# The FFN's up product as seven Strassen products, with weight parts formed on the fly

## The reference, cut to what matters

```python
def conv_glu_ffn(h, w_up, conv_w, conv_b, w_down):
    u = h @ w_up                       # 2048x1024 @ 1024x5632
    u = conv over 3 tokens, channel by channel, of u, + conv_b
    a, b = jnp.split(u, 2, axis=-1)    # 2816 channels each
    return (jax.nn.gelu(a, approximate=True) * b) @ w_down   # 2816x1024

x = x + rmsnorm(mix @ w_out, g_mix_post)
f = conv_glu_ffn(rmsnorm(x, g_ffn_pre), w_up, conv_w, conv_b, w_down)
x = x + rmsnorm(f, g_ffn_post)
```

## Time and profile before

| | us |
|---|---|
| median of 3 runs | 3394.72 (3394.04 to 3396.75) |
| profiled execution, its own time | 3392.44 |
| its span, first to last instruction | 3390.7 |
| PE busy | 3274.3 (97%) |
| DVE, ACT, POOL busy | 1412.9, 1190.6, 603.1 |
| mean granted TensorE clock | 0.989 |

### The profile page before, as it was taken

How to read it: one execution, slowest core, us unless ns; L and a number is a source line. 1 busy time by engine, 2 the same in 40 slices (tenths; PEclk the granted TensorE clock), 3 DMA queues, 4 the chain that set the end, 5 groups by cost and what they waited for, 6 DMA issues and landing times. The chain is left out here.

```text
span 3390.7 us, 46499 instructions
## 1 busy us (share of the span) xinstructions
PE 3274.3 (97%) x16834; PEld 2657.2 (78%) x16834; DVE 1412.9 (42%) x3866; ACT 1190.6 (35%) x2459; POOL 603.1 (18%) x551
## 2 busy tenths in 40 slices
PE   7999999998998989999999999999999999999998
PEld 6888888887776766666678878887888788888887
DVE  5111101105766977777744454304440344115421
ACT  5111111115666866666633343203330233013310
POOL 1566654530000014442110000000000000000000
PEclk9999999998999999999999999999999999999999
DMA  5789976657878833442247775646556655665553
GB/s 192 268 315 323 326 257 216 215 179 192 213 174 200 206 89 77 102 102 62 74 138 240 237 262 191 248 169 254 197 203 233 233 190 198 238 246 193 192 197 138
DMA packets 299259, 676.10 MB, mean 199 GB/s; under 512 B 99392, under 2 KB 154944, under 8 KB 284864
## 3 DMA queue, kind: packets, MB, share of 16 engines
q1 hardware_dynamic: 265344, 517.80, 48.0%
q0 software_dynamic: 33696, 155.40, 12.7%
HBM read 495.93 MB, written 185.57 MB: 201 GB/s over the span
## 5 line engine op out<-in xcount | busy, mean ns | idle before, releaser
L543 PE MATMUL z_banks<-h_hi,z_w_hi 128*128 128x512 f32 x972 | 381.2, 392 | 0.0
L543 PE MATMUL z_banks<-h_hi,z_w_lo 128*128 128x512 f32 x972 | 378.4, 389 | 0.0
L1640 PE MATMUL banks<-low,f_own 128*128 128x512 f32 x1344 | 312.6, 392 | 12.8 <-issue 6.6
L1640 PEld LDWEIGHTS banks<-low,f_own 128*128 128x128 f32 x1344 | 254.1, 189 | 67.2 <-issue 14.1
L1424 ACT ACTIVATE w_small<-w_small,a_stats 128x128 f32<-128x128 f32 (+3 forms) x510 | 257.1, 517 | 109.4 <-DVE a_stats L1510 80.8
L1354 PE MATMUL a_ot_ps<-a_turned_w,vs 128*64 128x256 f32 (+3 forms) x1452 | 221.3, 428 | 0.0
L1321 PE MATMUL a_t_ps<-idt,w_small 128*128 128x128 f32 x1092 | 216.2, 284 | 4.7 <-DVE a_turned_w L1413 2.6
L323 ACT ACTIVATE st_hi<-z_banks 128x512 fp32r<-128x512 f32 (+1 forms) x100 | 59.8, 598 | 444.2 <-PE z_banks L543 318.8
L461 DVE TENSOR_TENSOR st_lo<-z_banks,st_hi 128x512 fp32r<-128x512 f32 x76 | 52.3, 691 | 384.1 <-ACT st_hi L323 307.9
L543 PEld LDWEIGHTS z_banks<-h_hi,z_w_lo 128*128 128x128 f32 x972 | 182.6, 188 | 37.0
L543 PEld LDWEIGHTS z_banks<-h_hi,z_w_hi 128*128 128x128 f32 x972 | 182.7, 188 | 36.9
(11 more groups left out here) (263 smaller groups left out, 7081.9 us busy)
## 6 DMA issues: line engine op xcount, KB each, us to landing
f_own<-f_hi SPq DMA_DIRECT2D x88, 512.0 KB, 3.7
f_own<-f_lo SPq DMA_DIRECT2D x88, 512.0 KB, 4.6
z_xs<-in_w_ffn POOLq DMA_DIRECT2D x33, 1024.0 KB, 8.1
f_hi<-z_v_hi POOLq DMA_DIRECT2D x33, 1024.0 KB, 5.1
f_lo<-z_xs POOLq DMA_DIRECT2D x33, 1024.0 KB, 5.7
low<-z_hi SPq DMA_DIRECT2D x48, 512.0 KB, 7.7
k_hi<-f_hi SPq DMA_DIRECT2D x44, 512.0 KB, 3.6
k_hi<-f_lo SPq DMA_DIRECT2D x44, 512.0 KB, 4.5
```

The lines of the kernel that those rows point to most:

```text
L543: last = pe.matmul(banks[:, 4 * k + n, :], w[:, k, c, :], h[c][:, tok], start=(c == order[0] and q == 0), stop=(c == DC - 1 and q == 2))
L1640: last = pe.matmul(out, w[:, c * P:(c + 1) * P], rows[:, c, :], start=(c == 0 and x == 0), stop=(c == DC - 1 and x == 2))
```

## The change

- `split_v` and its DMAs leave `project`. `mix_out` and `ffn` become one function, `mix_ffn`, one block without loops in the program.
- The FFN goes through two halves of 1024 tokens (hf). Per channel tile, A is the 2x2 split of the weights (a or gate channels by upper or lower 512 of the model width) and B the 2x2 split of the tokens' rows (512 of width by 512 tokens). Seven products of 12 matmuls each take the place of eight (`PRODUCTS`). n = hf*22 + j numbers the channel tiles, so there are 44.
- For each n, GpSimd forms the four sums S1 to S4 of the raw weights and the lower parts of all seven operands, in eight instructions (`form`); ScalarE forms the upper parts in four. The raw 128x2048 tile comes by one DMA. The sums of rows T1 to T4 and their parts are formed once per half by VectorE and ScalarE.
- VectorE joins the products out of PSUM in five additions of 512 columns (`add_p6`, `add_p7`, `add_p5`, `take_c21`, `take_c12`), ScalarE copies P1 and C11. Taps, gelu and gate are as before, but 1024 columns long.
- Gated rows are stored in DRAM (`g_up`) and loaded again for the down product; w_down is loaded raw, and ScalarE and VectorE form the parts of both in each step (`split_down`). Six places, as before; the last two d, not four, are ordered by token tile.
- The rows h2 of tokens 1024 to 2047 go to DRAM unsplit (`h2_rest`) and are loaded by GpSimd in the first half's down product.

```diff
+PRODUCTS = ((0, A11, B11, True, 1, 1), (1, S2, T2, True, 2, 2), (0, A12, B21, False, 1, 3), (2, S3, T3, True, 3, 5),
+            (3, S1, T1, True, 3, 4), (2, A22, T4, False, 4, 6), (3, S4, B22, False, 4, 7))
...
+            def sums_a(n):
...
+                else:
+                    pool.wait_ge(p_done, 7 * (n - 1))
+                pool.tensor_tensor(lo[:, S1], raw[:, 2], raw[:, 3], ALU.add).then_inc(s_done, 1)
+                pool.tensor_tensor(lo[:, S3], raw[:, 0], raw[:, 2], ALU.subtract).then_inc(s_done, 1)
+                pool.wait_ge(s_done, 4 * n + 1)
+                pool.tensor_tensor(lo[:, S2], lo[:, S1], raw[:, 0], ALU.subtract).then_inc(s_done, 1)
...
+            def form(n):
+                raw = raws[n % 2]
+                sums_a(n)
+                lower_a(n, A11, 2, raw[:, 0:2], 1)
+                sum_b(n)
+                lower_a(n, S1, 2, None, 3)
+                lower_a(n, S3, 2, None, 4)
+                lower_a(n, A22, 1, raw[:, 3:4], 2)
...
+            for hf in range(2):
+                n0 = hf * NF
+                for n in range(n0 + (hf == 0), n0 + NF):
+                    last = n == n0 + NF - 1
+                    if not last:
+                        upper_a11(n + 1)
+                    if n > n0:
+                        last_tap(n - 1, 0, tap_a)
+                    take_p1(n)
+                    if n > n0:
+                        gelu(n - 1)
...
+                        upper_a22(n + 1)
+                        upper_s12(n + 1)
+                    take_c11(n)
...
+                        upper_s34(n + 1)
+                    last_tap(n, 1, tap_b)
...
+            def add_p7(n):
+                if n == 0:
+                    dve.wait_ge(h_turned, NT)
+                elif n == NF:
+                    dve.wait_ge(stored[1], 16 * TILES)
...
+                    if n > n0:
+                        tap(n - 1, 0, 1)
+                        tap(n - 1, 0, 0)
+                    add_p6(n)
+                    if n > n0:
+                        gate(n - 1)
...
+                    add_p7(n)
...
+                    add_p5(n)
...
+                    edge(n, 1)
...
+                    take_c21(n)
+                    tap(n, 1, 1)
+                    take_c12(n)
+                    edge(n, 0)
+                    tap(n, 1, 0)
...
+            def product(n, i):
...
+                if i == 2:
+                    pe.wait_ge(e1_done, n + 1)
+                elif i == 5:
+                    pe.wait_ge(ev_done, 5 * n + 2)
+                elif i == 6:
+                    pe.wait_ge(ev_done, 5 * n + 3)
+                w_hi, w_lo = a_hi(n, a)[:, 0, :], a_lo(n, a)[:, 0, :]
+                for c in range(4):
+                    for x, (w, rows) in enumerate(((w_hi, b_hi[b]), (w_lo, b_hi[b]), (w_hi, b_lo[b]))):
+                        last = pe.matmul(banks[:, 4 * (n % 2) + bank, :], w[:, c * P:(c + 1) * P], rows[:, c * 512:(c + 1) * 512],
```

The order at the two places where the FFN's halves begin. At the start (n = 0), ScalarE's queue and VectorE's queue around the last two token tiles of the mixer:

```diff
+                take_h(t - 1)
...
+                if t == NT - 1:
+                    upper_b(0, 2)
+                    upper_b(0, 3)
+                    upper_a11(0)
+                    upper_a22(0)
+                    upper_s12(0)
+                    upper_s34(0)
+            root_mix(NT - 1)
+            upper_b(0, 4)
+            take_p1(0)
+            root_x1(NT - 1)
...
+            act.wait_ge(h2_done, NT)
+            upper_b(0, 5)
+            take_c11(0)
+            upper_b(0, 6)
+            upper_a11(1)
...
+                if t == NT - 1:
+                    lower_b(0, 2)
+                    lower_b(0, 3)
+            to_x1(NT - 1)
+            lower_b(0, 4)
+            to_h2(NT - 1)
```

Between the halves, GpSimd's queue (q == 1, tiles t0 = 4 to 7, n = NF = 22):

```diff
+                        sums_a(NF)
+                        statistics(t0)
+                        lower_a(NF, A11, 2, raw[:, 0:2], 1)
+                        statistics(t0 + 1)
+                        sum_b(NF)
+                        lower_a(NF, S1, 2, None, 3)
+                        statistics(t0 + 2)
+                        lower_a(NF, S3, 2, None, 4)
+                        lower_a(NF, A22, 1, raw[:, 3:4], 2)
+                        store(t0)
+                        statistics(t0 + 3)
+                        for t in range(t0 + 1, t0 + TILES):
+                            store(t)
```

More of the change, by code:

```diff
@@ L1623, in _ @@
                     finish((n - 10) // 4)
[L1626 to L1642, removed]
@@ L1645, in mix_out @@
[L1645 to L1662 removed]
+NF = 22
@@ new lines @@
+LAST = 2
+TILES = 4
+SLOTS = 6
+HALF = T // 2
+STEPS = 2 * NF
+A11, A12, A22, S1, S2, S3, S4 = range(7)
+B11, T3, B21, B22, T1, T2, T4 = range(7)
+PRODUCTS = ((0, A11, B11, True, 1, 1), (1, S2, T2, True, 2, 2), (0, A12, B21, False, 1, 3), (2, S3, T3, True, 3, 5),
+            (3, S1, T1, True, 3, 4), (2, A22, T4, False, 4, 6), (3, S4, B22, False, 4, 7))
+SPLIT_ORDER = (B11, T2, B21, T1, T3, T4, B22)
+SUM_AT = {18: 0, 19: 1, 20: 2, 27: 3}
+UPPER_AT = {26: 0, 28: 1, 29: 2, 30: 3, 31: 4, 32: 5, 33: 6}
@@ L1976, in ffn @@
         rstd_done = sem("rstd_done")
+        gp_in = sem("gp_in")
+        r_in = [sem("r_in0"), sem("r_in1")]
         f_taken = sem("f_taken")
@@ L2016, in store @@
+                if t % 8 < 6:
                     pool.wait_ge(stored[t % 2], 16 * (t // 2) + 16)
                     load_x(t + 2)
[L2019 to L2035 removed]
+            split_lower(pool, 0)
@@ new lines, in project @@
+            def project(t):
+                k = t % 2
+                pe.wait_ge(ol_done, t + 1)
+                if t >= 2:
+                    pe.wait_ge(y_done, t - 1)
+                by_row = t in (0, NT - 1)
+                for n, c in [(n, c) for c in range(DC) for n in range(2)] if by_row else \
+                        [(n, c) for n in range(2) for c in range(DC)]:
+                    if t == 0 and n == 0:
+                        pe.wait_ge(wlo_done[c % 2], c // 2 + 1)
+                    for i, (part, w) in enumerate(((0, 0), (1, 0), (0, 1))):
+                        last = pe.matmul(mix[:, k, n * 512:(n + 1) * 512], oo[:, k, part, c, :], w_part(w, c)[:, n, :],
+                                         start=(c == 0 and i == 0), stop=(c == DC - 1 and i == 2))
+                    if t == NT - 1 and c == 3 and n == 1:
+                        last.then_inc(front_used, 1)
+                last.then_inc(mixed, 1)
@@ new lines, in _ @@
+            turn_o(0)
+            keep_turning(pe, banks[:, 6, :], idt, 16)
+            for t in range(NT):
+                if t + 1 < NT:
+                    turn_o(t + 1)
+                project(t)
+                if t:
+                    turn_h(t - 1)
+            for hf in range(2):
+                for n in range(hf * NF, hf * NF + NF):
+                    for i in range(7):
+                        product(n, i)
+                        if n == 0 and i == 3:
+                            turn_h(NT - 1)
+                for qq in range(2):
+                    down(hf, qq)
```

1125 lines of the change are left out of this document (668 added, 457 removed).

## The result

The changed kernel took 3315.88 us (median; 3312.45 to 3316.46), the kernel before beside it 3395.73. The ratio is 0.9762, 95% interval 0.9746 to 0.9779: 80 us faster, where 72 were forecast (3323 us). The profiled execution's span is 3310.7 us.

The account below looks back on a forecast made before the run. TensorE's queue, busy 97%, was taken as the bound. Matmuls -119.7, laps +21.2, start +14.1, between halves +8.0 and end +4.4 sum to -72.0, giving 3323 us; range 3286 to 3385.

Parts of the forecast that it names:

- its own sign of being wrong: Mid-half laps of 19.04 us, TensorE's own time for one n, would show the forecast of about 19.6 wrong.
- The matmuls: Up product: 528 fewer matmuls at 0.2267 us each, -119.7 us.
- the ring of 19.57 us: Up-product lap: turns of GpSimd, VectorE and ScalarE take 19.57 us against TensorE's 19.04, costing +21 us over forty laps.
- rival (a): Up-product laps: TensorE stays the bound in every lap, the turns fit in 19.04 us; 3292 us, chance 0.24.
- GpSimd's wait for ScalarE: Up-product lap: GpSimd idles 1.75 us for ScalarE's upper parts of A22 and S1/S2, with VectorE's gate running under it.
- The 0.5, 0.9, 1.4 us of growing lag: Up-product laps: GpSimd's S1 starts this far behind TensorE's product 0 in successive laps, until product 5 waits.
- the 4.8 and 4.9 us of lag: Start of each half: the next form late beyond the steady lag, 4.8 us in the first, 4.9 in the second.
- The start: FFN start: late operand parts, late next form and half clock lose 21.9 us, +14 us net.
- Between the halves: Turn between halves: add_p7 of n = 22 waits for tile 7's store; 8.4 us gap, 16.3 lost, +8 us net.
- The quarter boundaries: Down product: transfers and splits fit under its steps, taken as free, 0 us.
- The end: Kernel's end: only two last d in token order, so x1 of tile 15 is issued later, +4.4 us.
- The rival on the other side: Up-product laps: VectorE waits for a whole GpSimd operation each time, 22.0 us per lap, 3419 us; chance 0.12, or worse.

Follow-up runs that it names:

- e8: Changed kernel with product 0 of each n run twice (12 more matmuls, the first 12 overwritten): 3424.93 us, ratio 1.0092.
- e10: Changed kernel with two more GpSimd subtractions per form, and the taps' first operand read from PSUM except in each half's last n: 3313.73 us, ratio 0.9757.
- e6: Changed kernel with one more GpSimd subtraction of 512 columns in each of the 44 forms: 3345.36 us, ratio 0.9857.
- e7: Changed kernel with two more GpSimd subtractions in each form: 3406.33 us, ratio 1.0039 to the kernel before.
- e4: Changed kernel with ScalarE forming the first upper parts at the FFN's start before taking h2 of tile 14, not after: 3307.36 us, ratio 0.9749.
- e3: Changed kernel with GpSimd issuing stores of tiles 4 to 7 between the halves as soon as ready, x1 loads after the next lower part: 3305.10 us.
- e12: Changed kernel with the second half's third raw weight tile loaded only when the store of tile 7 has landed: 3309.35 us, ratio 0.9747.
- e2: Changed kernel with the down product's last four d, not two, in token order in all quarters but the second: 3303.32 us, ratio 0.9734.
- e9: Changed kernel with early upper parts, early stores, last four d by token, and the last tile's addition behind two splits at quarter boundaries: 3284.33 us.
- e11: Changed kernel with the second half's third raw weight tile loaded only when tile 7 is added up: 3313.54 us, ratio 0.9758.

## Why the prediction was right, and where its steps were not

The time came out 7 us under the forecast and inside the range, but the mechanism that the forecast rested on was not the one that ran: its own sign of being wrong, laps of 19.04, is what the trace shows. That the total fits is luck, as said above.

**The matmuls.** -119.7 us: right, and shown by the unbroken pieces and by e8, where the same number of matmuls, 528, cost 112.

**The lap.** The step that failed is the ring of 19.57 us; rival (a), laps of 19.04, is what the chip did. Its parts were good: GpSimd's 512 columns took 1.29 us (1.25 taken), the exclusion lengthens GpSimd's instruction by about 1.0 (1.15 taken), and e10 shows that it counts. In the changed kernel's lap the rows up to the end of S4 come to 10.2 us without the 0.5 of the fourth tap (10.29 in the sum), the wait for ScalarE to 1.5 (1.75) and the last three lower parts to 6.0 (6.1). What the sum had too long is its end: the last tap in full, 1.15, of which S1 felt 0.5, and the copies, 0.3, of which it felt nothing. Without its 0.8 us of waiting for TensorE the lap is 18.2 us.

Wrong above all was to hold GpSimd's wait for ScalarE (1.75 us, with the gate under it) fixed when GpSimd runs late. That wait exists while GpSimd is early. When it falls behind, the taps stand before other instructions of its own, the parts are ready when it comes, and 0.15 us of the wait are left (e6), while the gate comes to stand in GpSimd's way. So the bound is the sum that rival (a) named, GpSimd's instructions and VectorE's five, forecast at 18.5 and inferred from e6 and e7 as 18.4 (19.71 - 1.33). The 0.5, 0.9, 1.4 us of growing lag came from the same mistake. It cost the forecast all of the 21 us: of the 2.3 measured, 1.7 are the clock in 1973 to 1983. It also cost part of the 4.8 and 4.9 us of lag at the halves' begins.

**The start.** 18.0 lost, 21.9 forecast; product 0 began 10.7 us behind the last mixer matmul, forecast 10.8, and product 5 at 28.7, forecast 29.0. Right, for the reason given; e4 shows ScalarE's order to be it. The 3 us for half clock had no row behind them; the granted clock from 1932 to 1953 was 0.88, which is 2.5.

**Between the halves.** The mechanism (`add_p7` waits for the last store, GpSimd's lower parts stand before the stores) was right, by e3 with the reserve that a load moved with it. The gap was 15.7 us, not 8.4: 4.3 of it are the store beside the raw load (e12), for which I had taken 3.0 from a stretch without such a load. Another 2.2 are GpSimd's first store, which left 7.6 us behind the last down matmul (2614.64 and 2607.05), not 5.4; 0.8 are left over. The forecast's other terms, 4.9 of lag and 3 of clock, were too large: 3.8 of the 19.5 us lost lie outside the gap. So the sum was 19.5 for 16.3.

**The quarter boundaries.** Taken as free, 12.9 us measured: a missing term. The prediction priced the down product's transfers and splits, and said nothing of the scalings that free the banks. TensorE's 12.9 us are 9.1 of waits for the scalings of tiles 2 and 3 and about 1.8 at each boundary by the clock (0.94 in the 30 us from 2470 and from 3160). At the first boundary the scaling of tile 3 began at 2492.71, released by GpSimd's root, which stands in GpSimd's queue behind the store of tile 1 and the load of x1; by the program it also waits for the addition to tile 2. The shorter order by token (two d, not four) had been priced at the end of the kernel only. e2 shows both parts of it, and e9 that with one more edit the boundaries are free.

**The end.** +4.4 forecast, +6.4 measured: right in kind (e2).

**The rival on the other side** (VectorE behind a whole GpSimd operation each time) did not happen, but e7 shows how near it was: 2.6 us more on GpSimd per lap make the changed kernel 0.4% slower than the kernel before. Of the 2.5 us before the mixer's end I know no cause; they lie within the 6.2 us by which that point moves from trace to trace.

## What to carry to other kernels

When two engines exclude each other, add up one engine's instructions and the other's excluding ones per lap, and compare that sum with the bound engine's lap; a wait for a third engine did not belong to that sum here, because it shrank when the waiting engine was late. Before trusting a lap that fits, add one such instruction and look at what comes out. Fixed costs sit at the seams: there, follow every tile's store and load to the last one, and price a transfer by what runs beside it.

## What the runs showed of the hardware that I had not expected

VectorE's copy of two columns takes part in the exclusion. The copy and GpSimd's rows beside it in the changed kernel, behind the wait between the halves:

```profile
2637.52 2.37 POOL L1905 TENSOR_TENSOR f_wt<-f_wt_f,f_wt 128x1024 fp32r<-128x1024 f32 x1
...
2637.98 3.18 DVE L2296 COPY w_small<-near 128x2 f32<-128x2 f32 x1
...
2639.86 1.27 POOL L1897 TENSOR_TENSOR f_wt_f<-f_wt_f 128x512 f32<-128x512 f32 x1
```

The copy took 3.18 us and had taken 0.17 in the kernel before. It ended at 2641.16, 0.03 us behind the second of the two GpSimd instructions, so it did not get its turn between them. And a 512 KB store went from 3.0 us (e11, e12) to 7.2 beside a 1 MB load, so a transfer is priced by its neighbours. (The Trainium skill, SBUF — State Buffer, section "Who interferes with whom", names copies from SBUF to SBUF among the instructions that can take the port pair shared with GpSimd, for the whole instruction. By that rule, the trace agrees: the copy waited out the rest of one GpSimd instruction and the whole of the next, however short it is itself.)
